# Fourteen phases instead of twelve for the next pass's terms in a chunked recurrence on one core

## The reference, cut to what matters

```
def rwkv_dir_terms(r, k0, v, wl, al, w0, w2, a0, a2, k_k, k_a, r_k):
    w_log = -jax.nn.softplus(-(w0 + jnp.tanh(wl) @ w2)) - 0.5
    decay = jnp.exp(-jnp.exp(w_log))
    a = jax.nn.sigmoid(a0 + al @ a2)
    kk = hs(k0 * k_k)
    kk = kk / jnp.maximum(jnp.sqrt(jnp.sum(kk * kk, axis=-1, keepdims=True)), 1e-12)
    k = hs(k0 * (1.0 + (a - 1.0) * k_a))
    bonus = jnp.sum(rh * k * r_k, axis=-1, keepdims=True) * vh
    return rh, hs(decay), k, vh, kk, kk * hs(a), bonus

def step(s, inp):
    r_t, w_t, k_t, v_t, kk_t, b_t = inp
    sa = jnp.einsum('bhij,bhj->bhi', s, kk_t)
    s = s * w_t[:, :, None, :] - sa[..., None] * b_t[:, :, None, :] + v_t[..., None] * k_t[:, :, None, :]
    return s, jnp.einsum('bhij,bhj->bhi', s, r_t)
```

## Time and profile before

| what | value |
|---|---|
| median of 3 runs | 3141.71 us (3139.44 to 3145.6) |
| profiled execution, its own time | 3142.27 us |
| its span | 3140.5 us (1.77 us lie around it) |
| first busy matmul of the passes to the end of the recurrence | about 2069 to 2606 us in the span |
| PE, share of the span busy | 90% |
| DVE, ACT, POOL, share of the span busy | 58%, 37%, 33% |
| granted TensorE clock, mean of the span | 0.944 |

### The profile page before, as it was taken

How to read it: one execution, slowest core, us unless ns; L and a number is a source line. 1 busy time by engine, 2 the same in 40 slices (tenths; PEclk the granted TensorE clock), 3 DMA queues, 4 the chain that set the end, 5 groups by cost and what they waited for, 6 DMA issues and landing times. The chain is left out here.

```text
span 3140.5 us, 59085 instructions
## 1 busy us (share of the span) xinstructions
PE 2822.4 (90%) x25000; PEld 2224.9 (71%) x25000; DVE 1834.6 (58%) x2779; ACT 1153.8 (37%) x2127; POOL 1023.0 (33%) x582
## 2 busy tenths in 40 slices
PE   7999798999989998999999799978888887699987
PEld 4765576877867655767778587857777775479875
DVE  5878656886059786478840456466666644353062
ACT  4234434333142344343321522234455533332252
POOL 1422142544423211334444222244444430142202
PEclk8999999999999989999999899989999988799988
DMA  6322133433323211244332323220000004133111
GB/s 214 90 78 54 35 94 96 141 119 88 96 82 93 69 47 48 81 134 144 114 89 86 122 84 99 86 70 23 4 23 23 24 8 148 32 99 91 54 38 54
DMA packets 350230, 249.42 MB, mean 79 GB/s; under 512 B 10874, under 2 KB 322448, under 8 KB 349456
## 3 DMA queue, kind: packets, MB, share of 16 engines
q1 hardware_dynamic: 342704, 229.62, 24.2%
q10 hardware_dynamic: 7264, 16.03, 1.6%
HBM read 221.59 MB, written 16.52 MB: 76 GB/s over the span
## 5 line engine op out<-in xcount | busy, mean ns | idle before, releaser
L540 POOL TENSOR_TENSOR weights_lo<-weights_raw,weights_hi 128x1024 fp32r<-128x1024 f32 (+2 forms) x230 | 581.5, 2529 | 1114.5 <-ACT weights_hi L509 1114.5
L1179 PE MATMUL psum<-moving_hi,weights_hi 128*128 128x512 f32 x1472 | 601.6, 409 | 40.8 <-PEq L178 13.7
L1179 PE MATMUL psum<-moving_lo,weights_hi 128*128 128x512 f32 x1472 | 581.2, 395 | 0.0
L1179 PE MATMUL psum<-moving_hi,weights_lo 128*128 128x512 f32 x1472 | 580.7, 394 | 0.0
L1179 PEld LDWEIGHTS psum<-moving_hi,weights_hi 128*128 128x128 f32 x1472 | 280.7, 191 | 161.1 <-issue 68.0
L509 ACT ACTIVATE weights_hi<-weights_raw 128x1024 fp32r<-128x1024 f32 (+1 forms) x240 | 248.3, 1036 | 249.5 <-PE psum L1179 244.7
L1179 PEld LDWEIGHTS psum<-moving_hi,weights_lo 128*128 128x128 f32 x1472 | 280.8, 191 | 60.9
L1179 PEld LDWEIGHTS psum<-moving_lo,weights_hi 128*128 128x128 f32 x1472 | 281.8, 191 | 56.0 <-issue 3.8
L2596 POOL TENSOR_TENSOR second_off<-second_mats,second_masks 128x256 f32<-128x256 f32 x180 | 140.7, 786 | 154.8 <-PE psum L2059 154.1
L2652 PE MATMUL psum<-hn_hi,even_hi 128*128 128x256 f32 x480 | 166.4, 347 | 8.6 <-DVE hn_lo L1996 7.7
L2652 PE MATMUL psum<-hn_lo,even_hi 128*128 128x256 f32 x480 | 164.1, 342 | 0.0
(11 more groups left out here) (470 smaller groups left out, 6122.4 us busy)
## 6 DMA issues: line engine op xcount, KB each, us to landing
weights_raw<-in_w_up SPq DMA_DIRECT2D x88, 512.0 KB, 3.7
weights_raw<-in_w_in SPq DMA_DIRECT2D x80, 512.0 KB, 3.6
ada<-in_ada_w SPq DMA_DIRECT2D x9, 2048.0 KB, 9.4
odd_raw<-in_od_w_in SPq DMA_DIRECT2D x16, 1024.0 KB, 5.5
even_raw<-in_ev_w_in SPq DMA_DIRECT2D x30, 512.0 KB, 3.9
weights_raw<-in_w_down SPq DMA_DIRECT2D x32, 448.0 KB, 3.6
weights_raw<-in_w_o SPq DMA_DIRECT2D x16, 512.0 KB, 3.8
weights_raw<-in_w_down SPq DMA_DIRECT2D x16, 512.0 KB, 3.8
```

The source lines that it names most:

```text
L540: ops.tensor_tensor(self.ring.lo[i % n][:, a:b], self.ring.raw[:, t % self.ring.landing, a:b], self.ring.hi[i % n][:, a:b].bitcast(F32), A ...
L1179: return nc.tensor.matmul(to, (hi, lo)[which][:, at:at + P], moving(k)[part], start=start and k == 0 and i == 0, stop=stop and k == n_k - ...
```

## The change

`PHASES` goes from 12 to 14. Two phases that held two whole-row operations of DVE are split (e2 and e1; the two operations of `k`), and the two bonus operations of DVE are split too, so that a phase has at most one operation of DVE on whole rows. The other engines' parts get new phase numbers. With 14 phases over the same 21 places the place of most operations moves. Counted in rounds (round 0 is place 5):

| operation | place before | place after |
|---|---|---|
| second projection and sigmoid, running sum | 3 | 2 |
| e2 | 5 | 4 |
| e1 (d = 1) | 5 | 5 |
| three exponentials, norm product (d = 0), first operation of k | 6 | 7 |
| second operation of k | 6 | 8 |
| first bonus operation (d = 1) | 8 | 10 |
| second bonus operation (d = 1), normed key (d = 0) | 8 | 11 |
| bonus product (d = 1) | 10 | 13 |
| bonus times v (d = 1) | 12 | 14 |
| POOL's two products | 12, 15 | 11, 14 |
| decay, last three operations of DVE | 13, 17, 19, 20 | 13, 17, 19, 20 |

```
-            PHASES = 12
+            PHASES = 14
...
-                if phase == 3 and d == 0:
+                if phase == 4 and d == 0:
                     pe.wait_ge(self.a_ready, 1)
...
-                if phase == 5 and d == 1:
+                if phase == 8 and d == 1:
                     pe.wait_ge(self.a_ready, 1)
                     pe.wait_ge(self.bonus_in, 1)
...
-                if phase == 3:
+                if phase == 4:
                     act.wait_ge(self.sums_ready, self.n_sums)
...
-                        dve.wait_ge(self.sums_ready, 1)
-                        V.tensor_tensor(e1[:, :], e2[:, :], sg[:, :], ALU.add).then_inc(self.sums_ready, 1)
-                if phase == 3:
+                if phase == 3 and d == 1:
+                    dve.wait_ge(self.sums_ready, 1)
+                    V.tensor_tensor(e1[:, :], e2[:, :], sg[:, :], ALU.add).then_inc(self.sums_ready, 1)
+                if phase == 4:
                     dve.wait_ge(self.sums_ready, self.n_sums)
                     dve.wait_ge(self.a_ready, 1)
                     chain.then(V.tensor_scalar(self.k[:, :], a[:, :], col("k_a", p), omka[:, p:p + 1], ALU.mult, ALU.add))
+                if phase == 5:
                     if self.loads:
...
-                if phase == 4:
+                if phase == 6:
                     if d == 1:
                         dve.wait_ge(self.k_ready, 1)
                         dve.wait_ge(self.exps_ready, 1)
                         chain.then(V.tensor_tensor(cum[:, :], k_forward[:, :], sg[:, :], ALU.add))
+                if phase == 7:
+                    if d == 1:
...
-                if phase == 6 and d == 1:
+                if phase == 9 and d == 1:
...
-                if phase == 9:
+                if phase == 11:
...
-                if phase == 10:
+                if phase == 12:
...
-                if phase == 11:
+                if phase == 13:
```

More of the change, by code:

```diff
@@ L2314, in act @@
                     S.activation(e2[:, :], e2[:, :], ACT.Exp, scale=-DECAY).then_inc(self.exps_ready, 1)
-                if phase == 7:
+                if phase == 8:
                     whole = CH - 1 if d == 0 else 0
@@ L2350, in dve @@
                         chain.then(V.scalar_tensor_tensor(kk[:, :], k0, col("k_k", p), self.region, ALU.mult, ALU.mult))
-                if phase == 6 and d == 1:
+                if phase == 9 and d == 1:
                     dve.wait_ge(self.bonus_ready, 1)
                     V.tensor_tensor(o, self.region, v, ALU.mult)
-                if phase == 9:
+                if phase == 11:
                     dve.wait_ge(self.exps_ready, 2)
                     V.scalar_tensor_tensor(self.a_op, by_chunk(kk[:, :]), -1.0, by_chunk(e2[:, :]), ALU.mult, ALU.mult)
-                if phase == 10:
+                if phase == 12:
                     chain.then(V.tensor_tensor(a[:, :], kk[:, :], a[:, :], ALU.mult))
-                if phase == 11:
+                if phase == 13:
                     V.tensor_tensor(self.b_op, by_chunk(a[:, :]), by_chunk(e3[:, :]), ALU.mult)
             def pool(self, pool, phase):
-                if phase == 6:
+                if phase == 7:
                     if self.loads:
@@ L2367, in pool @@
                     G.tensor_tensor(self.r_op, by_chunk(r), by_chunk(e1[:, :]), ALU.mult)
-                if phase == 8:
+                if phase == 9:
                     pool.wait_ge(self.k_ready, 1)
```

## The result

| | before | after |
|---|---|---|
| median of 20 runs | 3139.99 us | 3146.11 us |
| ratio to before, 95% interval | | 1.0021 (1.0012 to 1.0029) |
| profiled execution's span | 3140.5 us | 3144.1 us |

The change makes the kernel slower by 0.2%, 6 us. Forecast were 3139 us, in a range of 3131 to 3146, and most likely no difference beyond 0.2%. The two profiled executions lie 3.6 us apart: that of before stands 2.3 us above the median of its 20 runs, that of after at its median.

The account below looks back on a forecast made before the run. PE was taken to set the pace, waiting on DVE and ACT, which end close together. Even passes -3.5, odd passes +1.0 and clock 0 gave -2.5 us: 3139 us against the median, range 3131 to 3146.

Parts of the forecast that it names:

- e2: DVE's whole-row operation, moved ahead of a state in even passes: its 1.27 us hidden, with 0.5 us to spare.
- What bounds the kernel now: PE sets the pace; at an even pass's first wait, ACT and DVE end within half a microsecond of each other.
- Even pass, sums and exponentials: e2 hidden, DVE's part of the first wait gone, but exponentials a round later: u begins +0.8 us later.
- Even pass, p(5): Bonus operations leave the stretch from u to the next p, replayed at 1.6 us: p comes 1.3 to 1.4 us earlier.
- Even pass, the two operations in later rounds: DVE's two bonus operations, now in rounds 5 and 6, cost 0.45 + 0.6, about +1.0 us an even pass.
- Bonus product: PE's product moves from round 5 to 8, away from the clock's fall: saves about 0.5 us in three of five even passes.
- Odd pass: Block starts later, u is copied about 0.2 us later, slack takes the normed key: +0.2 us each, +1.0 us for five.
- The clock: PE's granted clock over all passes: one odd fall more (+0.9 us) and one even fall less (-0.9 us), together 0.
- The sum: Whole kernel: -3.5 + 1.0 + 0 = -2.5 us on the profiled 3142.27, so 3139.8; against the median, 3139 us.
- The clock stays up: Rival: most even passes and the odd ones keep 2.4 GHz, eight falls go, 9.5 us less, 3132; chance 0.15.
- Both waits go: Rival: ACT's exponentials don't bind, PE gains 2.34 + 1.81 us in five even passes, about 3126; chance 0.07.
- The units collide: Rival: second projection and sigmoid don't fit into the units, rounds begin about 1.0 us later each pass, 3149; chance 0.12.

Follow-up runs that it names:

- the split: Three exponentials on places 6, 7 and 8 instead of one place: 3116.11 us on the changed kernel, 3127.62 us on the kernel before.
- Filled: Unread products added on PE ahead of its long waits: 3130.59 us on the changed kernel, 3127.16 us on the kernel before.
- the later bonus: Changed kernel with exponentials on three places and, in even passes' terms, second bonus operation, bonus product and its addition one place later: 3107.60 us.

## Why the prediction was wrong, step by step

The forecast had -4.4 us in the five even passes, one fall less included, and +1.9 in the odd ones, one fall more included. The profiles show -0.5 and +4.1. Three steps failed: the step from u(4) to p(5) was replayed at full clock, the two bonus operations were priced too low in their new rounds, and so was a fall of the clock in an odd pass.

The passes at a clock of 1.00 give one table, with all operations but the exponentials at the old or new places and the block of exponentials in three ways. Even pass, odd pass, us, each as most of the passes have it:

| places of the other operations | block at place 6 | block at place 7 | split from place 6 |
|---|---|---|---|
| before | 30.85, 29.56 | fallen in all passes | 30.88, 28.06 |
| after | 30.00, 29.47 | 31.02, 29.79 | 29.12, 28.28 |

The kernel before is the first cell, the changed one the middle of the lower row. The new places without the later block are worth 0.85 us of an even pass. That this is the regrouping of VectorE's operations is read from the two waits for `second_st`, which are gone; no run moves those operations without the other small moves (projection, norm product, POOL's products). The same renumbering moves the block a round later, and that takes 1.02 back.

- *What bounds the kernel now.* Right, and the heart of it: at the first wait VectorE and ScalarE end close to each other. In even passes the split is worth nothing at VectorE's old places and 0.88 us at the new ones; the regrouping is worth 0.85 us with the block where it was and 1.76 with the split. With the block a round later it gains nothing: 158.7 us in five even passes without it and 160.0 with it, both with falls.
- *Even pass, sums and exponentials.* Right. p was expected at 3.9 and came at 3.87; u(4) at 8.1 after a 3.2 us wait, and came at 8.16 after 3.31.
- *Even pass, p(5).* Right at one clock, wrong in the profile. Filled, p(5) comes at 9.80 against 11.00, 1.2 us gained of the 1.3 to 1.4 forecast. In after it comes at 10.48 to 10.75 in the four passes in which the fall lies on this step, and at 9.80 in the one in which it does not. The step was replayed with the 1.41 us of a stretch at full clock, though the same prediction put the falls in or behind such waits. This is one step that failed.
- *Even pass, the two operations in later rounds.* Mis-sized: +1.0 forecast. Filled, p(8) comes 10.62 us after p(5) in the changed kernel and 9.37 in the kernel before, +1.25, and 0.12 more by the end. With p(5) the even order gives +0.17 instead of the -0.4 forecast, 2.8 us in five passes, or 1.8 by the sums over all five: a second step that failed, in the size of a term.
- *Bonus product.* It does take 1.56 us again, but that 0.5 us was no gain of its own: the fall it had been in moved onto u(4) to p(5). Against the lengths at one clock, the five even passes of before lose 6.2 us and those of after 4.9; some 0.8 of the 6.2 are small delays of PE at full clock, as seen with filled waits too, in two passes. So the even falls cost about as much as before.
- *Odd pass.* Right at one clock, +0.23 where +0.2 was forecast. The normed key in round 6 took not quite the slack it was given: p(7) waits 0.24 us for the state there.
- *The clock.* Wrong in the odd passes, the third step that failed. One fall more was forecast, and one came, from three to four; but against the lengths at one clock the five passes of before lose 3.1 us and those of after 6.0, of this 1.1 to 1.7 in each fallen pass, where the earlier trace rows gave 0.9 to 1.3, and 0.3 in the pass that kept its clock. The forecast gain of an even fall did not come. On the rule of the Trainium skill ("TensorE: Matmul & The Clock Gate", section "HAM oscillation — how this bites in real kernels"), which says that long idle pieces between bursts put the array back to half rate, the runs agree as far as that the long wait of after fell in nine passes of ten and that filled waits kept the clock up in thirty of thirty; but the shorter waits of the kernel before fell in eight of ten as well, so the loss in the odd passes is in what a fall costs as much as in how many there are.
- *The sum.* By the profiles, even and odd passes: order +0.85 and +1.15, falls and delays -1.3 and +2.9, together +3.6, which is the difference of the two spans. With the sums over all filled passes in place of the usual lengths it is -0.2 and +1.4 for the order, -0.3 and +2.7 for the rest. Forecast were -2.0 and +1.0 for the order and -1.5 for the bonus product and clock.
- *Rivals.* "The clock stays up" had the right size for a kernel whose waits are filled (3127 to 3131), but the change lengthens the wait instead. "Both waits go" is what the split makes of it. "The units collide" did not happen: the first y product of this even pass waits 0.17 us instead of 0.42, and the odd one 0.60 as before; from the last term of an odd pass to the first y of the next even one it is 12.94 us instead of 12.88.

What stays open: why some passes with the same wait fall and others don't (the odd passes of before, one wait of 1.71 us each, fell three times in five; the split kernel with one of 1.41 us in its even passes never, and with the later bonus one odd pass fell about 1 us behind its first y, ahead of which PE had stood idle for no more than 0.97 us), and why the bonus operation took 1.38 us in its new round. It did so in three even passes of after, where two masks of POOL ran beside it for 1.0 us together, and took 1.00 in the two others, where they did for less than 0.1; but beside one mask for 0.8 us it took 1.02 in the kernel before. No run moves POOL's work alone.

## What to carry to other kernels

Where two engines end close together at one wait, price a move by what the second will do, and look for a change of both: here the regrouping (the exponentials left where they were) and the split were worth 0.15 and 0.31% alone and 0.85% together. A renumbering moves everything that is counted by it; look first at the longest block it carries along, and ask whether that block can be cut so that the short copies on which the next engine waits pass between its pieces. Replay a step behind a long PE wait at the clock that the trace shows behind such waits, not at full speed.

## What the runs showed of the hardware

- Work that nobody reads makes this kernel faster: 27 pairs of 64x64 products in the waits of each pair of passes took the kernel before from 3140.6 to 3127.2 us, with the granted clock at 1.00 in all ten passes. Of these 13 us 8 lie in the ten lengths.
- A fall of the clock costs an even pass some 0.4 to 1.5 us, and where it lies makes a difference: in the changed kernel, behind the same wait of 3.31 us, it cost 0.8 to 1.1 us on the step from u(4) to p(5) and 0.4 us one step later.
